# Delta rule scan with decays and key products loaded a step ahead by DMA, and blanking of the expert rows split over two stages

## The reference, cut to what matters

```python
def gated_delta_scan(q, k, v, g, beta, s0, with_output):
    qc, kc, vc = to_chunks(q), to_chunks(k), to_chunks(v)
    gc = jnp.cumsum(to_chunks(g), axis=-1)
    decay = jnp.exp(jnp.where(incl, gc[..., :, None] - gc[..., None, :], -jnp.inf))
    kb = kc * bc[..., None]
    lmat = jnp.where(pos[:, None] > pos[None, :], einsum('nbhid,nbhjd->nbhij', kb, kc) * decay, 0.0)
    rhs = jnp.concatenate([vc * bc[..., None], kb * jnp.exp(gc)[..., None]], axis=-1)
    sol = lax.linalg.triangular_solve(lmat, rhs, left_side=True, lower=True, unit_diagonal=True)
    ...
    def step(s, inp):
        v_new = u_i - jnp.einsum('bhcd,bhde->bhce', w_i, s)
        s_next = s * gl_i[..., None, None] + jnp.einsum('bhcd,bhce->bhde', kd_i, v_new)
        if with_output:
            o = jnp.einsum('bhcd,bhde->bhce', qd_i, s) + jnp.einsum('bhij,bhje->bhie', qk_i, v_new)
            return s_next, o
        return s_next, None
```

## Time and profile before

| | us |
|---|---|
| median of 3 runs | 4263.6 |
| lowest, highest | 4263.36, 4266.66 |
| the profiled execution | 4264.74 |
| its span | 4262.4 |
| TensorE busy | 3426.1 (80%) |
| VectorE busy | 1298.6 (30%) |
| ScalarE busy | 802.0 (19%) |
| GpSimd busy | 729.2 (17%) |
| mean granted TensorE clock | 0.888 |

### The profile page before, as it was taken

How to read it: one execution, slowest core, us unless ns; L and a number is a source line. 1 busy time by engine, 2 the same in 40 slices (tenths; PEclk the granted TensorE clock), 3 DMA queues, 4 the chain that set the end, 5 groups by cost and what they waited for, 6 DMA issues and landing times. The chain is left out here.

```text
span 4262.4 us, 61289 instructions
## 1 busy us (share of the span) xinstructions
PE 3426.1 (80%) x22370; PEld 2092.3 (49%) x22371; DVE 1298.6 (30%) x2473; ACT 802.0 (19%) x1857; POOL 729.2 (17%) x795
## 2 busy tenths in 40 slices
PE   4979898886688885994898866985858779999995
PEld 2458757834344442333454432441535346667662
DVE  2465484523100013114111013017445251111114
ACT  1432242210111111000111112110015112222221
POOL 0014204300211111000211110015200023333323
PEclk7989999987899997996999987988669889999997
DMA  7870011024599996324799985230020229998985
GB/s 262 215 158 1 2 44 28 1 100 186 212 419 411 408 381 241 143 103 169 305 396 419 416 363 217 110 119 0 1 72 1 85 107 365 382 368 321 345 345 197
DMA packets 170520, 896.99 MB, mean 210 GB/s; under 512 B 76376, under 2 KB 79002, under 8 KB 124315
## 3 DMA queue, kind: packets, MB, share of 16 engines
q1 hardware_dynamic: 110572, 740.62, 43.8%
q10 hardware_dynamic: 38196, 104.40, 8.0%
q0 software_dynamic: 21632, 50.37, 3.5%
HBM read 834.79 MB, written 82.54 MB: 215 GB/s over the span
## 5 line engine op out<-in xcount | busy, mean ns | idle before, releaser
L1949 PE MATMUL ps<-weight_ring,moe_xT 128*64 128x128 f32 (+1 forms) x2656 | 451.9, 331 | 68.8 <-DMA weight_ring<-in_w_dram 67.9
L1949 PE MATMUL ps<-moe_spare,moe_xT 128*64 128x128 f32 (+1 forms) x2528 | 418.0, 325 | 58.2 <-issue 58.2
L1951 PE MATMUL ps<-weight_ring,moe_xT 128*64 128x128 f32 (+1 forms) x2656 | 452.4, 331 | 0.0
L1949 PEld LDWEIGHTS ps<-weight_ring,moe_xT 128*64 128x64 f32 x2656 | 335.2, 143 | 216.0 <-DMA weight_ring<-in_w_dram 83.7
L1951 PE MATMUL ps<-moe_spare,moe_xT 128*64 128x128 f32 (+1 forms) x2592 | 437.2, 329 | 0.0
L2095 DVE TENSOR_TENSOR moe_act<-moe_sg,ps 64x128 f32<-64x128 f32 (+1 forms) x344 | 118.9, 346 | 1024.4 <-ACT moe_sg L2049 1024.4
L1949 PEld LDWEIGHTS ps<-moe_spare,moe_xT 128*64 128x64 f32 x2528 | 313.0, 140 | 168.2 <-issue 114.0
L1918 POOL COPY moe_xg<-moe_xin 64x1024 f32<-64x1024 f32 x172 | 177.3, 1031 | 1163.8 <-PE ps L1932 869.7
L1951 PEld LDWEIGHTS ps<-weight_ring,moe_xT 128*64 128x64 f32 x2656 | 334.2, 143 | 0.0
L1951 PEld LDWEIGHTS ps<-moe_spare,moe_xT 128*64 128x64 f32 x2592 | 322.3, 141 | 0.0
L2099 DVE COPY moe_y<-ps 128x512 f32<-128x512 f32 x172 | 118.9, 692 | 499.3 <-PE ps L1960 499.1
(11 more groups left out here) (635 smaller groups left out, 5079.8 us busy)
## 6 DMA issues: line engine op xcount, KB each, us to landing
weight_ring<-in_w_dram SPq DMA_DIRECT2D x96, 2048.0 KB
moe_spare<-in_w_dram SPq DMA_DIRECT2D x92, 2048.0 KB, 12.4
weight_ring<-in_w_exp_gu_dram SPq DMA_DIRECT2D x32, 2048.0 KB
moe_spare<-in_w_exp_gu_dram SPq DMA_DIRECT2D x32, 2048.0 KB
expert_rows<-moe_y ACTq DMA_DIRECT2D x344, 128.0 KB
moe_spare<-in_w_exp_dn_dram SPq DMA_DIRECT2D x16, 2048.0 KB
weight_ring<-in_w_exp_dn_dram SPq DMA_DIRECT2D x16, 2048.0 KB
expert_rows<-delta_o ACTq DMA_DIRECT2D x1, 25088.0 KB, 132.1
```

Source lines behind the costliest of these rows:

```text
L1949: nc.tensor.matmul(m.ps[0:UR, half, 0:W], xT[:, k, :], gate[:, k, cols], start=(k == 0), stop=(k == KD - 1))
L1951: last = nc.tensor.matmul(m.ps[UR:P, half, 0:W], xT[:, k, :], up[:, k, cols], start=(k == 0), stop=(k == KD - 1))
```

## The change

In `delta_heads`, the blanking now covers 18 units (E1 to UNITS1 + SENDS - 1) and is issued by SyncE as its first DMA; the other 80 units are blanked in `attention_stage`, where GpSimd clears a tile of zeros first and SyncE waits for the blanking before the stage's end. ScalarE copies each key product from PSUM to one of two SBUF buffers (`kk_kept`), SyncE stores it to device memory (`kk_there`), and `compact` reads the copy.

In `delta_scan`, SyncE loads for every step and direction the row of cumulated gates, broadcast to all partitions, into `L`, and the key products into `Tm`, as soon as the step before has done with these buffers. The matmuls L996 and L1003 go. `A` gets two buffers, and VectorE makes the next step's decay arguments before it copies this step's new values. The transposes of the inverse wait for it alone. The output from the state goes through `Z` in place of `X`.

The diff, cut to its core:

```diff
-def blank_rows(m, eng, zeros):
...
-    rows = m.expert_rows[E1 * UR:(UNITS2 + SENDS - 1) * UR, :].rearrange("(u p) d -> p u d", p=UR)
-    eng.dma_start(rows, across(zeros[0:UR, :], UNITS2 + SENDS - 1 - E1)).then_inc(m.rows_blank, 16)
+def blank_rows(m, sp, zeros, u0, u1):
...
+    rows = m.expert_rows[u0 * UR:u1 * UR, :].rearrange("(u p) d -> p u d", p=UR)
+    sp.dma_start(rows, across(zeros[0:UR, :], u1 - u0)).then_inc(m.rows_blank, 16)
...
         def _(sp):
+            if hg == 0:
+                blank_rows(m, sp, p.o[:, 0, :], E1, UNITS1 + SENDS - 1)
             sp.wait_ge(s.gates_moved, 1)
...
             for j in range(2):
+                for t in range(3 * j, 3 * j + 3):
+                    sp.wait_ge(s.kk_moved, t + 1)
+                    sp.dma_start(p.kk_there[t], kk_kept[:, t % 2, :]).then_inc(kk_out[t % 2], 16)
                 sp.wait_ge(s.compact, 3 * j + 3)
...
+                    for t in kk_units.get(u, []):
+                        act.wait_ge(s.kk, t + 1)
+                        if t >= 2:
+                            act.wait_ge(kk_out[t % 2], 16 * (t // 2))
+                            act.wait_ge(s.masked, t - 1)
+                        nc.scalar.activation(kk_kept[:, t % 2, :], kk_bank(t), ACT.Copy).then_inc(s.kk_moved, 1)
...
+        @block.sync
+        def _(sp):
+            gates = p.g_there.rearrange("(x d t h) c -> x d t (h c)", x=2, d=2, h=4)
+            for i in range(steps):
+                for d in range(2):
+                    e, b, t = S2[d], B[d], order[d][i]
+                    if i:
+                        sp.wait_ge(e.lm, LV * i)
+                    sp.dma_start(b["L"], gates[0, d, t].partition_broadcast(P)).then_inc(e.gcb_in, 16)
+                for d in range(2):
+                    e, b, t = S2[d], B[d], order[d][i]
+                    if i:
+                        sp.wait_ge(e.z, LV * i)
+                    sp.dma_start(b["Tm"], p.kk_there[t]).then_inc(e.kk_in, 16)
...
+            def decay_args(i, d):
+                e, b, t = S2[d], B[d], order[d][i]
+                dve.wait_ge(e.gcb_in, 16 * (i + 1))
+                if t >= NCT:
+                    dve.wait_ge(e.a_v, latents(i - 1))
+                    nc.vector.tensor_tensor(h3(A(i, d)), h3(b["L"]), across(p.masks[:, 4 + d, :], 4),
+                                            ALU.add).then_inc(e.argB, 1)
+                    dve.wait_ge(e.argB, latents(i) + 1)
+                nc.vector.scalar_tensor_tensor(out=h3(b["L"]), in0=h3(b["L"]), scalar=-1.0,
+                                               in1=across(p.masks[:, 2 + d, :], 4),
+                                               op0=ALU.mult, op1=ALU.add).then_inc(e.argA, 1)
...
+            def lower(i, d):
+                e, b, t = S2[d], B[d], order[d][i]
+                dve.wait_ge(e.expA, i + 1)
+                dve.wait_ge(e.kk_in, 16 * (i + 1))
+                for h in range(4):
+                    j = 8 * d + 4 * hg + h
+                    last = nc.vector.scalar_tensor_tensor(out=hd(b["L"], h), in0=hd(b["L"], h),
+                                                          scalar=p.beta[:, t, j:j + 1], in1=hd(b["Tm"], h),
+                                                          op0=ALU.mult, op1=ALU.mult)
+                last.then_inc(e.lower, 1)
...
+            for i in range(steps):
+                for d in range(2):
+                    level_mask(i, 0, d)
+                for d in range(2):
+                    gated(i, d)
+                for l in range(1, LV):
+                    for d in range(2):
+                        level_mask(i, l, d)
...
+            for i in range(steps):
+                more = i + 1 < steps
+                for d in range(2):
+                    attention(i, d)
+                for l in range(LV):
+                    for d in range(2):
+                        merge(i, l, d)
+                    if l == 0:
+                        for d in range(2):
+                            unseen(i, d)
+                if more:
+                    for d in range(2):
+                        decay_args(i + 1, d)
+                for d in range(2):
+                    new_values(i, d)
+                if more:
+                    for d in range(2):
+                        expand(i + 1, d)
+                for d in range(2):
+                    new_state(i, d)
+                for d in range(2):
+                    from_state(i, d)
+                if more:
+                    for d in range(2):
+                        lower(i + 1, d)
+                for d in range(2):
+                    output(i, d)
...
+            blank_rows(m, sp, zeros, UNITS1 + SENDS - 1, UNITS2 + SENDS - 1)
+            sp.wait_ge(m.rows_blank, 32)
```

More of the change, by code:

```diff
@@ L699, in _ @@
             sp.wait_ge(s.x_in, 32)
+            for t in range(2):
+                sp.wait_ge(kk_out[t], 16 * nt // 2)
         @block.gpsimd
@@ L1045, in level_pq @@
                 if l < XL:
+                    pe.wait_ge(e.o_done, latents(i))
                     for h in range(4):
@@ L1049, in level_pq @@
                 last.then_inc(e.pq, 1)
-            def keys_on_state(i, d):
-                e, b, c = S2[d], B[d], cols(order[d][i])
-                pe.wait_ge(e.zero, 1)
-                pe.wait_ge(e.state, i)
-                for h in range(4):
-                    last = nc.tensor.matmul(hd(bank(d, 3), h), p.kT[:, h, c:c + P], hd(b["S"], h),
-                                            start=True, stop=True)
-                last.then_inc(e.k_s, 1)
             def values(i, d):
@@ L1098, in _ @@
                     keys_on_state(i, d)
-                for d in range(2):
-                    first_level(i, d)
                 for l in range(LV):
@@ new lines, in attention, with unseen @@
+            def attention(i, d):
+                e, t = S2[d], order[d][i]
+                if t >= NCT:
+                    dve.wait_ge(e.expB, latents(i) + 1)
+                    dve.wait_ge(e.qk, latents(i) + 1)
+                    nc.vector.tensor_tensor(A(i, d), A(i, d), bank(d, 1), ALU.mult).then_inc(e.attn, 1)
+            def unseen(i, d):
+                e, b, t = S2[d], B[d], order[d][i]
+                dve.wait_ge(e.k_s, i + 1)
+                dve.wait_ge(e.bv, i + 1)
+                for h in range(4):
+                    j = 8 * d + 4 * hg + h
+                    last = nc.vector.scalar_tensor_tensor(out=hd(b["bV"], h), in0=hd(bank(d, 3), h),
+                                                          scalar=p.nbege[:, t, j:j + 1], in1=hd(b["bV"], h),
+                                                          op0=ALU.mult, op1=ALU.add)
+                last.then_inc(e.unseen, 1)
@@ L1223, in _ @@
-                for d in range(2):
-                    e, b, t = S2[d], B[d], order[d][i]
-                    dve.wait_ge(e.k_s, i + 1)
-                    dve.wait_ge(e.bv, i + 1)
-                    for h in range(4):
-                        j = 8 * d + 4 * hg + h
-                        last = nc.vector.scalar_tensor_tensor(out=hd(b["bV"], h), in0=hd(bank(d, 3), h),
-                                                              scalar=p.nbege[:, t, j:j + 1], in1=hd(b["bV"], h),
-                                                              op0=ALU.mult, op1=ALU.add)
-                    last.then_inc(e.unseen, 1)
+                    attention(i, d)
```

307 lines of the change are left out of this document (144 added, 163 removed).

## The result

| | before | after |
|---|---|---|
| median of the runs | 4265.1 us (4 runs) | 4199.7 us (4 runs) |
| lowest, highest | 4263.4, 4276.4 | 4190.0, 4212.9 |
| ratio after to before | | 0.9843, 95% interval 0.9809 to 0.9877 |
| the profiled execution, its span | 4264.7, 4262.4 | 4195.1, 4193.1 |
| TensorE busy, mean granted clock | 3426.1 (80%), 0.888 | 3372.5 (80%), 0.889 |

The account below looks back on a forecast made before the run. It took the first projection to wait on a store held by the blanking, and the scan on TensorE's work, waits and slow clock: 4264.7 - 14.0 - 61.6 = 4189 us, range 4168 to 4213.

Parts of the forecast that it names:

- Blanking: First projection: with only 18 units blanked there, VectorE's 14.0 us wait for the key product reload goes, -14.0 us.
- sentence "0": Projections: the added copies and stores of the key products cost nothing, with 15.7 us of cover before VectorE needs the reload.
- The walk through the scan: Instruction-by-instruction timing of each engine through a scan: 171.7 us against 202.5, -30.8 for each of two scans.
- step 0 to 1, 1 to 2: Scan's early steps, between TensorE's products for the values: 24.9 and 26.3 us, or 23.9 and 25.3 if unblocked.
- second update starts: TensorE's update for the second direction starts at V+5.9 us, V being the step's mark, the product for the values.
- late steps: Last three mark-to-mark steps of each scan: 29.0 us each, against 37.6 for three before; 27.5 if unblocked.
- rival 2: Scan: TensorE's waits still bring a slow clock in each late step, 23 us for both scans, 4212 us; chance 0.14.
- A late step has 30 of them: Scan before the change: 30 groups of eight short matmuls plus 0.93 of transposes, 27.6 us; the other 10 waits and slow clock.
- The fork: VectorE in the scan: whether `lower`, with two SBUF inputs, is blocked by GpSimd; blocked was taken, 171.7 us against 165.2 unblocked.
- rival 1: Scan: `lower` isn't blocked by GpSimd, late steps take 27.5 us and the kernel 4176 us; chance 0.24.
- Rival 3: First projection doesn't gain, since key product stores replace the blanking in holding the compact store; 4203 us, chance 0.06.
- Rival 4: Scan: gate loads land late, each us beyond 7.1 costing one per step over ten steps; slower than before, chance 0.03.

Follow-up runs that it names:

- the blanking alone: Kernel before with only the blanking split, 18 units by SyncE in the first projection and 80 in the attention stage: median 4253.6 us, ratio 0.9966.
- the repeat: The changed kernel run again without any edit: median 4197.4 us, ratio 0.9839 to the kernel before.
- late gates: Changed kernel with the next step's gates loaded when the product for the values is done, instead of after the last level mask: 4273.8 us.

## Why the prediction was right, and where not

The forecast was -75.6 us for the stages, the measured -72.8: -14.6, -28.7 and -28.5 for the terms that it names, and -1.1 for the second projection, which it had at nothing. That one took 148.9 us before, 148.8 with the blanking alone and 147.8 now, so it comes with the copies and stores of the key products; what in them gives it is open. With 3.5 us lost outside the four stages the profiled execution is 6.0 above the forecast.

**Blanking**, -14.0: right in the mechanism and the size, shown by the blanking alone (-13.1). It landed 25.5 us after its issue (24 forecast). The attention blanking took 106.3 (108 forecast) and cost nothing. What the text didn't see is that the key product stores made the split necessary: its sentence "0" for these stores holds only because the blanking is short.

**The walk through the scan**, -30.8 each:

| | forecast | measured (first scan) |
|---|---|---|
| start to first mark | 25.0 | 25.6 |
| step 0 to 1, 1 to 2 | 24.9, 26.3 | 24.5, 26.5 |
| second update starts | V+5.9 | V+5.8 |
| `lower` of direction 1 ends | V+12.3 | V+11.9 |
| levels start | V+16.2 | V+15.7 |
| late steps | 29.0 x3 | 28.7, 31.4, 28.7 |
| tail | 8.5 | 8.5 |

Without a slow clock in the late steps the scans measure 170.5 and 171.5 against 171.7. The mis-sized term is the one that the sum has at zero: the slow clock, put aside as rival 2 for "each late step". It is not all or nothing. It fell in one late step of three in each scan of that profile, 2.7 us each, 5.4 in all against the rival's 23, and in none of the repeat. The 0.5 us by which the levels start earlier are `lower`'s end, 0.4 early, and the four output sums, 3.0 us where the walk has 3.2.

**"A late step has 30 of them"** was a miscount: the kernel before has 32 groups in one, 28.6 us, and 0.9 of transposes; the changed one has 28. It entered no sum, but it made waits and slow clock look like 10 us where they were 8.1.

**The fork**: `lower` is blocked, as taken (2.15 us for four, 1.1 with GpSimd idle). The Trainium skill, "SBUF — State Buffer", section "Who interferes with whom", states this for any VectorE instruction with two SBUF inputs beside one of GpSimd that reads SBUF; this run now shows it for a scalar_tensor_tensor, one of four at 1364 ns, where 351 is the longest with GpSimd idle. But rival 1's price, 1.5 us a late step, stays untested: with the block removed by a later mask the step was 28.9. What `lower` would give with neither the block nor the later mask wasn't tried.

**Rival 3** did not occur (stores 2.0 to 4.0 us to landing, no wait). **Rival 4** did not either, with landings of 3.0 to 4.2 under 7.1 us of cover; but its price, one us per us, was too low: late gates cost 6.7 us a step for a wait of 4.3, 1.6 per us, with slow groups behind the wait.

## What to carry over

When a change takes work from the busiest engine, put the work back as idle instructions: here 3.6 us of it cost 1.3, which showed that the hand-overs bound the step and how much is left in them. Then move what frees a buffer or a bank ahead of what only sums, and use the engine beside it in the gaps where it blocks nobody; one such move alone shifted the wait to the next engine, all together gave 1.9 us a step. Before new DMAs go into an ordered queue, look for what already makes that queue wait.

## What the runs showed of the hardware

**The clock can fall behind short, scattered waits.** In late steps with TensorE waits of 0.6 and 0.8 us close together, groups spaced by 1.7 us instead of 0.9, as at 1.2 instead of 2.4 GHz, followed in 4 of 24 (four profiles of the changed order); with 0.5, 1.0 and 0.8 in 4 of 6; with 0.2 and 1.1 in 4 of 6; with two of 2.1 to 2.5 in 5 of 6; with 0.5, 0.5 and 0.5 in none of 6; with one of 4.5 in all 6, with one of 3.4 in all 12 of the two kernels with the old scan; with none over 0.3 in none of 12. Where steps with and without a fall stand in one run, it cost 1.1 to 4.8 us. What decides between identical steps is open.

**A store in small pieces landed only when a large write did, stores in long rows before it didn't wait so long.** Beside the 25,088 KB the compact store of 96 KB, in pieces of 64 bytes, took 40.6 us, the product stores of 256 KB, in rows of 2 KB, 13.6 at most. That the piece's size is the cause wasn't separated from their order in the queue. The Trainium skill, "DMA: Bandwidth & Descriptors", section "Queues, rings and completion order", has each DMA engine take turns between queues, a whole packet of descriptors at a time. If so, a queue of small pieces would move fewer bytes in a turn; that would fit, and no run here tests it.

**Code that nobody touched varies as much as many effects here.** From TensorE's first group of the output projection to its first of the compression stage in the third block the thirteen profiles show 2197.9 to 2214.7 us, though no edit touches what lies between. The 23 runs of the kernel before that stand beside four of the experiments spread from 4252.9 to 4282.7, so a window of a changed stage tells in one profile what a median hardly does.
